# A decoder trunk on one core: the turn and the square of layer 1 put ahead of a step's first sample

## The reference, cut to what matters

```
S, y = scan(x, dt, a, B, C, S)        # the state and the scan's outputs
y = (y + d_skip * x) * silu(z)        # skip and gate
y = y * rsqrt(mean(y*y over the 512 columns of the unit) + eps)
out += (y * w_norm) @ w_out           # the unit's share of the output projection
```

```
S[b] = exp(dt*A) * S[b] + (dt*x[b]) outer B[b]
y[b] = S[b] . C[b]
```

## Time and profile before

| | |
|---|---|
| median of 3 runs | 1471.96 us (1471.08 to 1472.51) |
| the profiled execution | 1473.36 us |
| its span in the profile | 1471.6 us |
| TensorE busy | 1408.5 us, 96% |
| VectorE busy | 1164.2 us, 79% |
| ScalarE busy | 839.9 us, 57% |
| mean granted TensorE clock | 0.991 |

### The profile page before, as it was taken

The page is one execution under the profiler, slowest core; times in us unless marked ns, Lnnn a source line. Parts: engine busy times, 40 slices in busy tenths (PEclk is TensorE's granted clock), DMA queues, the critical chain, the costliest instruction groups (busy, mean ns, idle before and its releaser), DMA issues. The chain is left out here.

```text
span 1471.6 us, 31302 instructions
## 1 busy us (share of the span) xinstructions
PE 1408.5 (96%) x11554; PEld 1173.3 (80%) x11554; DVE 1164.2 (79%) x2591; ACT 839.9 (57%) x1877; POOL 235.6 (16%) x424
## 2 busy tenths in 40 slices
PE   6999999999999989998999999999999999999987
PEld 6999897767888779987888888877777777787765
DVE  4567687767878987889897898986979788488786
ACT  5755644476566555556665754654657465555553
POOL 6010111011321101121120220120012110000003
PEclk9999999999999999999999999999999999999999
DMA  7485657356676345267845754852575674554453
GB/s 209 125 258 163 193 137 218 103 163 186 156 217 182 100 150 161 84 149 226 270 121 155 252 145 128 240 142 84 181 240 147 179 203 124 175 169 154 140 188 65
DMA packets 283874, 245.77 MB, mean 167 GB/s; under 512 B 32664, under 2 KB 250876, under 8 KB 283052
## 3 DMA queue, kind: packets, MB, share of 16 engines
q1 hardware_dynamic: 273628, 209.36, 48.1%
q0 software_dynamic: 10096, 34.41, 8.7%
HBM read 183.02 MB, written 65.00 MB: 169 GB/s over the span
## 5 line engine op out<-in xcount | busy, mean ns | idle before, releaser
L1514 PE MATMUL bank<-h,w 128*128 128x268 f32 (+1 forms) x4752 | 829.1, 328 | 8.7 <-ACT w L893 3.6
L1514 PEld LDWEIGHTS bank<-h,w 128*128 128x128 f32 x4752 | 695.2, 190 | 85.0 <-issue 12.1
L909 DVE TENSOR_TENSOR w<-w_raw,w 128x1024 fp32r<-128x1024 f32 x132 | 160.9, 1219 | 39.8 <-ACT w L893 39.6
L878 PE MATMUL bank<-s_w_out,s_yt_hi 128*128 128x512 f32 (+2 forms) x544 | 168.0, 398 | 1.7 <-DVE s_ys L2632 1.0
L893 ACT ACTIVATE w<-w_raw 128x1024 fp32r<-128x1024 f32 x132 | 138.8, 1051 | 11.8 <-DMA w_raw<-in_ssd_w_in_dram 7.3
L1592 DVE SCALAR_TENSOR_TENSOR conv<-before_conv,cw,conv 128x260 f32<-128x260 f32 (+2 forms) x216 | 125.2, 580 | 4.3
L878 PEld LDWEIGHTS bank<-s_w_out,s_yt_hi 128*128 128x128 f32 (+2 forms) x544 | 95.9, 180 | 28.1 <-issue 2.1
L878 PE MATMUL bank<-g_w_out,g_ot_hi 128*128 128x512 f32 (+2 forms) x288 | 95.7, 420 | 1.7 <-DVE g_ot_lo L2150 1.7
L878 PE MATMUL bank<-s_w_out,s_yt_lo 128*128 128x512 f32 x240 | 94.7, 395 | 0.0
L2395 ACT ACTIVATE s_decay<-s_decay,t_ac 128x128 f32<-128x128 f32 (+1 forms) x288 | 85.5, 379 | 1.2
L2714 ACT ACTIVATE s_yt_hi<-bank 128x512 fp32r<-128x512 f32 (+1 forms) x36 | 20.1, 558 | 115.7 <-PE bank L2705 115.5
(11 more groups left out here) (259 smaller groups left out, 2446.9 us busy)
## 6 DMA issues: line engine op xcount, KB each, us to landing
w_raw<-in_ssd_w_in_dram SPq DMA_DIRECT2D x80, 512.0 KB, 4.3
w_raw<-in_gla_w_in_dram SPq DMA_DIRECT2D x48, 512.0 KB, 4.6
s_decay<-kept_acd SPq DMA_DIRECT2D x32, 512.0 KB, 6.1
w_raw<-in_ssd_w_out_dram SPq DMA_DIRECT2D x30, 512.0 KB, 4.1
g_chunk<-kept_gq SPq DMA_DIRECT2D x32, 448.0 KB, 5.6
s_chunk<-kept_sq SPq DMA_DIRECT2D x32, 384.0 KB, 4.8
kept_sq<-stage SPq DMA_DIRECT2D x80, 134.0 KB, 4.6
kept_sq<-stage SPq DMA_DIRECT2D x40, 256.0 KB, 4.8
```

What stands on the lines that cost most here:

```text
L878: last = pe.matmul(bank[0:r, :], yt[a][:, k, 0:r], wo[:, b, 512 * half:512 * half + 512], start=(k + a + b == 0), stop=(k == tiles - 1 and ...
L909: dve.tensor_tensor(self.part(i, 1), self.raw(i), hi, ALU.subtract).then_inc(self.w_lo, 1)
L1514: last = pe.matmul(bank[:, 0:n], w[:, p.tile % 2, a, k, :], h[:, b, k, c:c + n], start=(i == 0), stop=(i == len(terms) - 1))
```

## The change

`("turn", 0), ("square", 0)` are moved in `step` from behind `("sample", 0), ("fill", 0.6)` to the place in front of `("sample", 0)`, behind `("spread", 0), ("fill", 0.1)`. The fill shares keep their places and sizes, so the parts of pieces between the other tasks stay as they were. No instruction is added or removed.

```diff
         step = [("decay", 1), ("scan", 0), ("fill", 0.6), ("lows",), ("weight", 1), ("fill", 0.5), ("gates", 0),
                 ("load", 2), ("lows",), ("fill", 0.4), ("norm", 0), ("inputs", 1), ("products", -1),
-                ("weight", 2), ("fill", 0.4), ("lows",), ("spread", 0), ("fill", 0.1), ("sample", 0), ("fill", 0.6), ("turn", 0), ("square", 0), ("weight", 3),
+                ("weight", 2), ("fill", 0.4), ("lows",), ("spread", 0), ("fill", 0.1), ("turn", 0), ("square", 0),
+                ("sample", 0), ("fill", 0.6), ("weight", 3),
                 ("r_add", -2), ("r_in", -1), ("fill", 0.3), ("lows",), ("sample", 1), ("fill", 0.4),
                 ("r_square", -1), ("r_out", -2), ("fill", 0.3)]
```

## The result

The changed kernel takes 1482.66 us (median of 4 runs, 1481.8 to 1483.83), the kernel before 1472.24 us (4 runs, the three known ahead of the prediction and one of 1476.33). The ratio is 1.0064, 95% interval 1.0051 to 1.0077: slower by 9.4 us by the ratio, 10.4 us by the medians. The forecast was 1475.4 us, slower by 3.4 us. The direction was right, the size was under half of what came, and the time lies outside the range of 1468.2 to 1480.5.

What follows compares the result with a forecast made beforehand. TensorE was taken as the bound, busy 436.6 of 450 us in the changed stage. Terms 2.5 + 1.7 - 1.0 + 0 - 0.6 + 0.8 gave +3.4 us, so 1475.4 us, range 1468.2 to 1480.5.

Steps and rivals of the forecast that it cites:

- The three stalls: TensorE's waits at the scan's first product for the turn's low part, 6.0 us together, which the change would remove.
- ScalarE's place in line: The sample's scaling on ScalarE now comes behind TensorE's transposes and the turn's copy and square, making VectorE's state update late.
- Unit 1, step 2: The late scaling moves the state update from 862.36 to 865.0, so TensorE waits at the z turns: +2.5 us.
- unit 0, step 2: Scaling done at 737.65 instead of 735.4; the delay lands at z turns that already waited 1.23 us: +1.7 us.
- the stall of unit 2: In step 2, the 3.11 us stall goes but the state update comes about 1.1 us later; idleness changes place: 0 us.
- Unit 1, step 3: The scan starts 1.77 us earlier, but the state update still ends at 883.39, limiting the gain: -1.0 us.
- Unit 3: VectorE's delays in steps 2 and 3 land at z turns that already wait 0.40 us: +0.8 us together.
- The first steps: Step 1 of units 0, 1 and 2: nothing in TensorE's list of waits depends on them, 0 us each.
- the steps set to 0: The three steps 1, unit 2's step 3 and the four steps 4: no TensorE wait hangs on them, 0 each.
- rival (c): ScalarE's place costs more: 7 steps with 1 to 2.7 us each, plus the clock; 1482 us, chance 0.13.
- no wait for a weight: Weight loads wait for VectorE's lows, up to 2 us later, but two more weights lie ahead: 0 us.
- Rival (a): The scan's stalls stay gone as VectorE makes up delays before the z turns: -6.0 us, 1466.0 or 1468, chance 0.21.

Runs made afterwards that it cites:

- between sample and fill: The kernel before, with turn and square moved directly behind the first sample and ahead of the fill of 0.6: 1473.3 us, ratio 0.9991.

## Why the prediction was right and wrong

**Right: the bound and the stalls.** The three stalls were waits for the low part and went, 6.0 to 0.6 us; the transposes on TensorE are free (0.9998 with them alone); no wait of TensorE that ends with GpSimd or with a load shows.

**Right: the mechanism on ScalarE.** The forecast named ScalarE's place in line as the price. Putting the scaling back ahead takes the ratio from 1.0064 to 1.0007. Unit 1, step 2 was worked out as +2.5 and measured +2.7; unit 0, step 2 as +1.7 and +2.1; the stall of unit 2 changed its place as said. Unit 1, step 3 was -1.0 and measured -1.0, with some luck: the same order gave 22.20 us, +0.2, in the version without the move in step 4. Unit 3 was +0.8 and came out at +0.2. The first steps were set to 0 and came out between -1.0 (unit 1) and +0.5; these are not explained. Of the steps set to 0 four have a sample, where the text counts five; the sum does not hang on it.

**Wrong: the sum left the clock out.** The forecast mentions the clock only in rival (c), "at about 1 us each", and gives that rival 0.13. By its own terms it should have been in the sum: the wait that it forecast at the z turns of unit 0 was 1.23 + 1.7 = 2.9 us, and in unit 2 it moved a stall of 3.1 us and added a delay of 1.1. The z turns waited 3.37 and 4.32 us there. These rows, and behind them the windows of 5 us from each on, are of the changed kernel:

```profile
749.19 0.63 PE L2676 MATMUL bank<-ident,s_z 128*128 128x128 f32 x4 [3.37 <-DVE states L2621]
...
977.71 1.09 PE L2676 MATMUL bank<-ident,s_z 128*128 128x128 f32 x4 [4.32 <-DVE states L2621]
```

```profile
749.19:754.19 5.00, 5.00 (x26) 4.77 (x27) 4.44 (x12) 1.51 (x4) 0.00 (x0) 0.66 1.08 248
977.71:982.71 5.00, 5.00 (x24) 5.00 (x25) 4.92 (x9) 1.47 (x3) 0.00 (x0) 0.50 0.21 81
```

Behind each wait TensorE was busy without a gap and ran at 1.2 GHz for some microseconds. By the windows this cost about 5 x 0.34 = 1.7 us in unit 0 and 5 x 0.50 = 2.5 us in unit 2. By TensorE's busy time in the whole step, against the kernel before, it is 22.48 - 20.95 = 1.5 and 23.61 - 21.45 = 2.2 us, 3.7 together. The excess of the table over the forecast in these two third steps is 1.9 + 1.6 = 3.5. That the clock is what makes these steps long is shown by the two versions with added matmuls, which bring the busy time back with the clock.

The kernel before had paid for its stall of 3.11 us too: 5 x 0.16 + 5 x 0.18 = 1.7 us, from the window in the earlier trace rows and the next one:

```profile
970.00:975.00 5.00, 4.90 (x87) 4.40 (x79) 4.86 (x9) 2.94 (x7) 0.00 (x0) 0.82 0.54 122
```

That price stood in unit 2, step 2. It is mostly gone there, but this step is not shorter for it, since now VectorE's late state update ends it. The low clock now follows the z turns, behind which TensorE has a long run of work, and there it is paid in full. A term for it could be had from these rows alone: two waits forecast at 2.9 and 4.2 us, priced at 1.7 us each like the stall of 3.11, are an estimate of 3.4 us, and the forecast would have stood near 1479. In rival (c) it was "about 1 us each"; it measured 1.5 and 2.2.

The Trainium skill, "TensorE: Matmul & The Clock Gate", section "Part 1: The HAM clock gate", says that the throttled state is the default; the trace agrees (0.50 behind the wait of 4.32 us).

The low clock is still the smaller part of the loss. Over the 16 steps TensorE's idle time grew by 6.8 us (13.3 to 20.1) and its busy time by 1.5, since the low clock of before in unit 0, step 1 and unit 2, step 2 became shorter while the new one came.

**Wrong: one delay, one wait.** A late state update was charged once, at the z turns. The output products stand behind it on the sum of the outputs; this wait returned in the last step of units 0 and 1, about 0.5 us each, where the forecast had 0.

**Wrong: no wait for a weight.** The forecast counted 0 for the weights and named a weight that comes too late as a sign of being wrong. In unit 2, step 4 this came, 0.6 us: not loaded too late but rounded too late, by a ScalarE that stood at the turn's copy. It is the mechanism of the forecast, in a step without a sample.

The fourth steps are 1.7 us together. With 3.5 and 1.7 the sum of 3.4 becomes 8.6, against 8.3 in the table; the small differences of the other steps make up the rest.

**Rival (a), and the rule behind it,** that what releases the most-contended engine's gaps should start sooner, did not hold here even with its cost taken away. With the scaling first the release came sooner and the time stayed (1.0007). The gap had a second release right behind the first, the state update. The sum of the two waits tells it: 9.1 us before, 9.1 with the scaling first, 9.8 between sample and fill, and all three within 0.2% in time. With the z turns later the sum fell to 3.8 and 4.4 us, and the time stayed even so, with waits at other lines. The Trainium skill, "Perfetto Trace Analysis", section "Optimization Strategy", says to make such a release start sooner; this is not refuted here, but the next release has to be priced with it.

## What to carry to other kernels

An engine with much idle time may be early and not idle: its place in line is what its customers live on. Before an instruction that waits for the slowest engine is moved ahead of others, count what the engine had done in the time in which it would now stand. When a stall of the bounding engine ends with one semaphore, look for the next wait on the same late engine and price the gain to there. And a long wait of TensorE, here 3.4 and 4.3 us, belongs in the sum with the low clock that stands behind it in the trace.

## What the runs showed of the hardware that was not expected

A float32 matmul of 128x128 by 128 columns was recorded as two instructions in the added matmuls: 18 gave 36 instructions and 4.2 us, 8 gave 16 and 1.95 us. Added work ahead of a wait kept the clock up behind it and made the step that follows shorter: 21.8 against 23.3 us in unit 0. Whether the program as a whole gains is not settled (ratios 1.0046 and 1.0064, with intervals that overlap).

The same wait does not always bring the low clock. In unit 1 the z turns waited 2.60 us at 867.58 in the changed kernel and 2.62 us at 866.70 with steps 1 to 3 alone changed. These are the 5 us from there on, in this order:

```profile
867.58:872.58 5.00, 5.00 (x33) 4.61 (x34) 4.93 (x11) 1.61 (x4) 0.00 (x0) 1.00 0.60 164
```

```profile
866.70:871.70 5.00, 5.00 (x27) 4.87 (x28) 4.93 (x11) 1.62 (x4) 0.00 (x0) 0.66 0.62 169
```

The step behind it took 21.03 us in the one and 22.20 in the other.
